# Gathering an expert pair's tokens with the selection stationary: 512-column moves, a copy, and eight transposes between the down matmuls

## What is computed

```python
def moe(h, router_w, router_b, w_gu, b_gu, w_d, b_d):
    tok = h.reshape(-1, D_MODEL)                       # 288 tokens, D_MODEL = 1024
    top_v, top_i = lax.top_k(tok @ router_w + router_b, 4)     # 4 of 32 experts
    gates = einsum(softmax(top_v), one_hot(top_i, 32))
    def expert(acc, xs):
        wgu, bgu, wd, bd, g = xs                       # (1024, 2048) and (1024, 1024), fp32
        u = tok @ wgu + bgu
        glu = minimum(u[:, ::2], 7.0); lin = clip(u[:, 1::2], -7.0, 7.0)
        a = glu * sigmoid(1.702 * glu) * (lin + 1.0)
        return acc + g[:, None] * (a @ wd + bd), None
```

## Time and profile before

| what | value |
|---|---|
| median of the runs | 1317.4 us (three runs, 1314.9 to 1321.56) |
| the profiled execution's own time | 1313.23 us |
| its span, first to last instruction | 1311.3 us |
| TensorE busy | 1222.4 us, 93% of the span |
| VectorE, ScalarE busy | 387.0 us, 232.3 us |
| DMA moved | 500.64 MB, mean 382 GB/s |
| mean granted TensorE clock | 0.972 |

### The profile page before, as it was taken

How to read it: one execution, slowest core, us unless ns; L and a number is a source line. 1 busy time by engine, 2 the same in 40 slices (tenths; PEclk the granted TensorE clock), 3 DMA queues, 4 the chain that set the end, 5 groups by cost and what they waited for, 6 DMA issues and landing times.

```text
span 1311.3 us, 17401 instructions
## 1 busy us (share of the span) xinstructions
PE 1222.4 (93%) x7250; PEld 515.3 (39%) x7250; DVE 387.0 (30%) x551; ACT 232.3 (18%) x528; POOL 117.6 (9%) x117
## 2 busy tenths in 40 slices
PE   7999887658999999999999999999999999999996
PEld 3455443323553443434434343343434343343431
DVE  5999962205232211111211112211111112111113
ACT  3021141201421111101112011111201011211102
POOL 2222335263100000000000000000000000000000
PEclk8999998778999999999999999999999999999999
DMA  9999857873889999999999999999999999999994
GB/s 344 387 345 369 319 168 243 304 257 136 328 329 414 430 428 427 429 428 429 428 428 429 428 428 429 428 429 427 429 429 428 430 427 430 428 428 429 426 428 191
DMA packets 56316, 500.64 MB, mean 382 GB/s; under 512 B 6329, under 2 KB 6609, under 8 KB 27601
## 3 DMA queue, kind: packets, MB, share of 16 engines
q1 hardware_dynamic: 41840, 430.55, 78.4%
q0 software_dynamic: 14432, 69.47, 14.5%
HBM read 495.29 MB, written 4.72 MB: 381 GB/s over the span
## 4 chain that ended last, share of the span: by engine, by line
PE 59%; DMA 25%; DVE 9%; issue 5%; ACT 2%; POOL 1%; another core or an unknown queue 0%; SPq 0%; DVEq 0%; POOLq 0%; ACTq 0%
PE psum L904 22%; DMA arena<-w_gate_up 21%; PE psum L935 12%; DVE arena L1379 6%; PE psum L854 4%; PE psum L836 3%; DMA arena<-w_down 3%; PE psum L574 2%; PE psum L488 2%; PE psum L866 2%; PE psum L682 2%; PE psum L414 1%; PE psum L873 1%; PE psum L842 1%; POOL arena L1845 1%
## 5 line engine op out<-in xcount | busy, mean ns | idle before, releaser
L904 PE MATMUL psum<-arena 128*64 128x512 f32 x1920 | 422.7, 594 | 15.1 <-DMA arena<-w_gate_up 15.1
L904 PEld LDWEIGHTS psum<-arena 128*64 128x64 f32 x1920 | 134.9, 137 | 299.3 <-issue 264.6
L1699 DVE TENSOR_SCALAR arena<-psum 128x512 f32<-128x512 f32 x32 | 22.1, 692 | 682.2 <-PE psum L904 642.9
L935 PE MATMUL psum<-arena 128*64 128x512 f32 x960 | 212.6, 595 | 0.0
L1052 ACT ACTIVATE arena<-psum 64x512 f32<-64x512 f32 (+3 forms) x185 | 94.0, 510 | 406.1 <-PE psum L935 170.7
L1379 DVE STREAM_TRANSPOSE arena<-arena 128x2048 f32<-128x2048 f32 x32 | 121.6, 3946 | 2.7 <-PE psum L474 2.4
L935 PEld LDWEIGHTS psum<-arena 128*64 128x64 f32 x960 | 66.4, 137 | 124.1 <-issue 122.3
L488 PE MATMUL psum<-arena 128*128 128x512 f32 x224 | 107.2, 617 | 0.5 <-issue 0.4
L1270 ACT ACTIVATE arena<-arena 128x512 f32<-128x512 f32 x30 | 18.9, 631 | 418.8 <-DVE arena L1699 418.8
L1052 ACT ACTIVATE arena<-psum,arena 128x128 f32<-128x128 f32 (+2 forms) x182 | 53.8, 398 | 179.2 <-PE psum L488 124.6
L836 PE MATMUL psum<-arena 128*128 128x128 f32 x512 | 77.2, 294 | 0.0
(11 more groups left out here) (224 smaller groups left out, 733.0 us busy)
## 6 DMA issues: line engine op xcount, KB each, us to landing
arena<-w_gate_up SPq DMA_DIRECT2D x128, 2048.0 KB, 29.7
arena<-w_down SPq DMA_DIRECT2D x64, 2048.0 KB, 33.4
arena<-w_in SPq DMA_DIRECT2D x7, 2048.0 KB, 21.2
arena<-w_out SPq DMA_DIRECT2D x2, 2048.0 KB, 9.7
out<-arena SPq DMA_DIRECT2D x4, 512.0 KB, 2.6
out<-arena POOLq DMA_DIRECT2D x1, 2048.0 KB, 13.0
arena<-x_prompt SPq DMA_DIRECT2D x2, 512.0 KB, 4.7
arena<-cache_v,arena POOLq DMA_INDIRECT x64
```

Source lines behind the costliest of these rows:

```text
L904: last = mm(psum[64 * g:64 * (g + 1), b, :], xt[:, 2 * kk + m, lhs], gate_slot[slot][:, m, c:c + 512], start=False, stop=kk == 3 and m == ...
L935: last = mm(psum[64 * g:64 * (g + 1), 2, :], at_sb[:, m, SLOTS * q:SLOTS * (q + 1)], down_slot[slot][:, m, 512 * g:512 * (g + 1)], start=q ...
```

## The change

`gather` now keeps `sel` stationary and moves `hn` in 512 columns: one call per 128-token tile, two matmuls each, and in the second call two more matmuls for the 32-row tile. The result in banks 6 and 7 is slot by feature, so it has to be turned: ScalarE copies the 1024 columns to a new SBUF tile `xg_sb`, and `turn_x` transposes it in eight blocks of 128 (with the same stride of two) back into banks 6 and 7, from where the eight scaled copies to `xt` go on as before. In `pair`, `turn_x(n + 1)` stands after expert 1's first down part, and after that part's `w_used`. Ahead of pair 0, and in the extra rounds (the `Fori` over `more`, which this data does not enter), it stands right behind the gather.

```diff
+        xg_sb = at(Q + 1242, D)
...
-            def gather(n, kk):
+            def gather(n, tile):
 
                 pe.wait_ge(sel_ready, n + 1)
-                for m in range(2):
-                    for bank in range(2):
-                        cols = slice(512 * bank + 256 * kk + m, 512 * bank + 256 * (kk + 1), 2)
-                        o = psum[:, 6 + bank, P * (2 * kk + m):P * (2 * kk + m + 1)]
-                        for tile in range(2):
-                            mm(o, hn[:, tile, cols], sel[:, tile].rearrange("p a b -> p (a b)"),
-                               start=tile == 0, stop=False, skip_group_check=True)
-                    for bank in range(2):
...
-                        last = mm(o, hn[rows, 2, cols], sel[rows, 2].rearrange("p a b -> p (a b)"),
-                                  start=False, stop=True, skip_group_check=True)
-                if kk == 1:
-                    last.then_inc(xt_full, 1)
+                for half in range(2):
+                    mm(psum[:, 6 + half, :], sel[:, tile].rearrange("p a b -> p (a b)"),
+                       hn[:, tile, 512 * half:512 * (half + 1)], start=tile == 0, stop=False)
+                if tile == 1:
+                    for half in range(2):
+                        rows = slice(NS * half, NS * (half + 1))
+                        last = mm(psum[:, 6 + half, :], sel[rows, 2].rearrange("p a b -> p (a b)"),
+                                  hn[rows, 2, 512 * half:512 * (half + 1)], start=False, stop=True)
+                    last.then_inc(xg_full, 1)
+
+            def turn_x(n):
+
+                pe.wait_ge(xg_ready, n + 1)
+                for kk in range(2):
+                    for m in range(2):
+                        for half in range(2):
+                            cols = slice(512 * half + 256 * kk + m, 512 * half + 256 * (kk + 1), 2)
+                            last = tr(psum[:, 6 + half, P * (2 * kk + m):P * (2 * kk + m + 1)],
+                                      xg_sb[:, cols], ident)
+                last.then_inc(xt_full, 1)
...
                         last.then_inc(w_used, 1)
+                        if ahead and e == 1 and q == 0:
+                            turn_x(n + 1)
...
             gather(0, 0)
             gather(0, 1)
+            turn_x(0)
...
             def gathered(n):
+                act.wait_ge(xg_full, n + 1)
+                copy(xg_sb, psum[:, 6:8, :].rearrange("p a b -> p (a b)")).then_inc(xg_ready, 1)
                 act.wait_ge(xt_full, n + 1)
```

More of the change, by code:

```diff
@@ L380, in build_kernel @@
             "sel_ready", "selg_ready", "xt_full", "xt_ready"))
-        picked_ready = sem("picked_ready")
+        picked_ready, xg_full, xg_ready = map(sem, ("picked_ready", "xg_full", "xg_ready"))
         sq_ready, f_rstd, yo_ready, stored = map(sem, ("sq_ready", "f_rstd", "yo_ready", "stored"))
@@ L825, in _ @@
             count(2, ones, 1, start=False, stop=True).then_inc(rank_full, 1)
-            def gather(n, kk):
+            def gather(n, tile):
                 pe.wait_ge(sel_ready, n + 1)
-                for m in range(2):
-                    for bank in range(2):
-                        cols = slice(512 * bank + 256 * kk + m, 512 * bank + 256 * (kk + 1), 2)
-                        o = psum[:, 6 + bank, P * (2 * kk + m):P * (2 * kk + m + 1)]
-                        for tile in range(2):
-                            mm(o, hn[:, tile, cols], sel[:, tile].rearrange("p a b -> p (a b)"),
-                               start=tile == 0, stop=False, skip_group_check=True)
-                    for bank in range(2):
-                        cols = slice(512 * bank + 256 * kk + m, 512 * bank + 256 * (kk + 1), 2)
-                        o = psum[:, 6 + bank, P * (2 * kk + m):P * (2 * kk + m + 1)]
-                        rows = slice(NS * bank, NS * (bank + 1))
-                        last = mm(o, hn[rows, 2, cols], sel[rows, 2].rearrange("p a b -> p (a b)"),
-                                  start=False, stop=True, skip_group_check=True)
-                if kk == 1:
-                    last.then_inc(xt_full, 1)
+                for half in range(2):
[16 more added lines that the diff above has]
+                last.then_inc(xt_full, 1)
             def combine(m, units):
@@ L1033, in _ @@
                     gather(n, 1)
+                    turn_x(n)
                     pair(n, in_extra(n), False)
```

## The result

| | before | after |
|---|---|---|
| median of the runs | 1317.4 us (7 runs, 1314.9 to 1321.56) | 1323.06 us (7 runs, 1320.58 to 1327.41) |
| ratio | | 1.0042, 95% interval 1.0023 to 1.0062 |
| span of the profiled execution | 1311.3 us | 1319.0 us |

The kernel became slower by 0.42%; 5.7 us lie between the medians, and the forecast was 1.2 us. I compare three stretches: the front (first gather to first bias), the stage (first bias to the end of the last down part) and the tail (from there to the end of the span). Of the 7.7 us between the two spans, 3.0 lie ahead of the first gather, none in the front, 1.0 in the stage and 3.7 in the tail.

What follows compares the result with a forecast made beforehand. The weights' DMA stream was taken as the bound, with TensorE's +0.9 us a pair hidden; only the 1.2 us delay ahead of pair 0 counted, 1317.4 + 1.2 = 1318.6 us, range 1313 to 1325.

Steps and rivals of the forecast that it cites:

- The bound: Expert stage: the weights' DMA stream sets the end, 184 parts x 4.89 us = 900 us, a pair every 58.73 us.
- The sum per pair: TensorE in the stage: -0.6 + 1.36 + 0.1 = +0.9 us, so 56.9 us a pair.
- the wait for VectorE: Stage, `turn_a` after the shorter tile 0: a new TensorE wait of about 1.1 us per pair.
- 32-row matmuls: Second gather call: the two small matmuls cost 0.95 us if side by side, at most 1.74 in a row.
- transposes: Eight in `turn_x`: +1.36 us on TensorE per pair, at most 2.3.
- A drain at the change of tile shape: Around the 32-row matmuls: switching tiling mode drains TensorE, possibly some tenths of a us more; the terms took nothing from it.
- The room: Stage: TensorE may take up to 57.6 us a pair before setting the end; 1.6 us of room, 0.9 used.
- The front: Ahead of pair 0: nothing covers the round trip, so first release and DMA stream come 1.2 us later (+0.8 to +2.0).
- The clock: Rival, ahead of pair 0: a new 1.3 us gap drops TensorE to 1.2 GHz, about 1321 us; chance 0.14.
- TensorE as the bound: Rival, stage: 32-row matmuls in a row with stops at shape changes, 57.7 us a pair, about 1321; chance 0.13.
- DMA earlier: Rival, ahead of pair 0: gather, copy and transposes beat 6.7 us; at best 1312 us, 0.4% less; chance 0.05.
- Sum: 1313.23 + 1.2: Whole kernel: the profiled execution's 1313.23 us plus the 1.2 us delay ahead of pair 0 gives 1314.4 us.

Runs made afterwards that it cites:

- a_load1: Changed kernel plus one filler matmul of 512 columns per pair, ahead of expert 1's down parts; ratio to the kernel before 1.0036, stage 918.1 us.
- a_load3: Changed kernel plus three filler matmuls per pair, ahead of expert 1's down parts; ratio to the kernel before 1.0218, stage 943.9 us.

## Why the prediction was right, and where it was not

The time lies in the stated range (1313 to 1325) and within 0.5% of before. In part that is luck: the amount is not what the sum gave, the range reached so high for the sake of two rivals that did not happen, and the case that made the difference was none of the forecast's.

**The bound.** Right. DMA runs at 428 GB/s, and the stage takes 914.6 to 915.7 us in every kernel whose pairs stay under 57.7, whatever TensorE does. Once the chain has turned to DMA, pairs repeat every 58.76 us (chain pieces at 1018.76 and 1077.52), the 58.7 that 12 parts take.

**The sum per pair.** Predicted 56.9, measured 56.83. Its terms: the wait for VectorE 1.1 predicted, 0.93 idle; 32-row matmuls 0.95, measured 1.06 and side by side; transposes 1.36, measured 1.14; `turn_x` without a wait. A drain at the change of tile shape has at most the 0.19 us that 1.06 is above the 0.87 of a side-by-side pair.

**The room.** The threshold of 57.6 holds. With 48.9 us for the last pair (the prediction had 50; this is fitted to a_load1), 1.0 + 15 x 57.88 + 48.9 = 918.1, and the same sum for a_load3, 1.0 + 15 x 59.60 + 48.9 = 943.9, is what it measured; 914.7 corresponds to 57.65. The chain turned to DMA at 961 us, not 1030.

**The front.** The mechanism is right, the size not: 1.2 us predicted, 0.5 measured at full clock on both sides (10.14 and 10.62). From the start of the gather to the last transpose the prediction had 7.9 us, 0.5 of it for slow clock; measured are 6.84 at full clock (373.97 to 380.81), since the eight transposes take 1.05 instead of 1.36 and the copy with both handovers 1.1 instead of 1.2 to 1.6.

**The rivals.** *The clock* didn't fall behind the first gather in the changed kernel; the fall ahead of it, found in both kernels, is worth more than anything the change does there. *TensorE as the bound* didn't happen, but a_load1 shows how near it was: 1 us more a pair, and the stage is 3.4 us longer and the kernel 0.36% slower (0.19 to 0.52). *DMA earlier* didn't happen.

**The step that failed** is "Sum: 1313.23 + 1.2": it took the front for the only term and passed over the tail, since none of its instructions was touched. The tail measured +3.7 to +4.5 us. With the front's 0.5 this gives 4.2 to 5.0 of the 5.7 us between the medians; the rest is inside the interval. Without the tail's second wait the changed kernel measures 0.9995 (0.9975 to 1.0016): the wider gather and its round trip are worth nothing that these times can show, though the interval has room for the front's 0.5 us, and for 1.2.

## What to carry to other kernels

Where a transfer is the bound of a long stage, ask of an edit only three things: does it move the start of the stream, does it open a pause in it, does it lengthen what comes behind it. Matmul time inside the stage is free up to a sharp edge, and the edge can be worked out from the rows ahead of time. An edit that removes instructions also moves all code behind it. If a jump over a seldom-used body stands shortly before the end, look at the sequencer's rows around it in both profiles before a few microseconds are put down to the edit.

## What was not expected of the hardware

- The place of code in TensorE's program was worth 3.7 to 4.8 us at the end of this kernel, and 24 instructions that are never executed removed it. The stop ends 1.2 to 1.3 us behind the landing of a 16,384-byte instruction packet.
- The second stop also costs clock: around the end of 4.0 to 4.4 us without a matmul the granted clock fell to 0.50, for 3.4 us in three profiles and 6.8 in one.
- Beside a gap of 1.45 us in which TensorE waited for VectorE, thirteen profiles of thirteen have 3.4 to 10.2 us at 1.2 GHz. Two filler matmuls in its place left the clock at 2.4 GHz in the one profile taken, and with the new order took 0.3% off the time.
